# A third modulation piece is computed ahead of the attention, and its weight blocks move ahead of the output projection's

## The reference, cut to what matters

```
m = silu(cond) @ w_mod[l] + b_mod[l]            # (6 x 1024): m0..m5
h = x * (1 + m1) + m0
x = layer_norm(ALPHA * x + m2 * attention(h))
h = x * (1 + m4) + m3
x = layer_norm(ALPHA * x + m5 * moe(h))
```

## Time and profile before

| | us |
|---|---|
| Timed runs, median of 3 | 919.88 (914.09 to 920.38) |
| Profiled execution | 915.48 |
| Its span (first to last instruction) | 913.7 |
| TensorE busy, matmuls | 812.9 (89%) |
| VectorE busy | 277.4 (30%) |
| Transfers | 276.86 MB, mean 303 GB/s |

### The profile page before, as it was taken

The page is one execution under the profiler, slowest core; times in us unless marked ns, Lnnn a source line. Parts: engine busy times, 40 slices in busy tenths (PEclk is TensorE's granted clock), DMA queues, the critical chain, the costliest instruction groups (busy, mean ns, idle before and its releaser), DMA issues.

```text
span 913.7 us, 10159 instructions
## 1 busy us (share of the span) xinstructions
PE 812.9 (89%) x3883; PEld 396.2 (43%) x3883; DVE 277.4 (30%) x551; ACT 147.2 (16%) x384; POOL 82.3 (9%) x166
## 2 busy tenths in 40 slices
PE   3897988989899999999899957997789999999985
PEld 1454554464343434343234724546434443444321
DVE  0004444661121212221242074557112211221126
ACT  0201222231110111010021112323101010111101
POOL 0000000005110111000000030000511011100000
PEclk9798799999999999999999977997899999999998
DMA  8999902199979999999997099102098999999901
GB/s 314 352 356 401 387 30 92 64 410 422 369 312 421 412 416 420 425 416 417 387 365 263 14 411 422 66 32 93 2 366 331 424 411 422 408 428 418 376 0 47
DMA packets 66955, 276.86 MB, mean 303 GB/s; under 512 B 4668, under 2 KB 11324, under 8 KB 58724
## 3 DMA queue, kind: packets, MB, share of 16 engines
q1 hardware_dynamic: 65764, 275.59, 76.0%
q10 hardware_dynamic: 1152, 0.74, 0.3%
HBM read 274.79 MB, written 1.52 MB: 302 GB/s over the span
## 4 chain that ended last, share of the span: by engine, by line
PE 81%; DVE 9%; ACT 5%; DMA 2%; issue 2%; SPq 1%; POOL 1%; POOLq 0%; ACTq 0%; DVEq 0%
PE bank L952 24%; PE bank L1013 13%; PE bank L700 8%; PE bank L926 6%; PE bank L960 5%; PE bank L787 5%; PE bank L634 4%; PE bank L735 3%; DMA ring<-in_w_mod 2%; PE bank L613 2%; PE bank L766 2%; DVE arena L1410 2%; PE bank L744 2%; ACT arena L1469 1%; PE bank L934 1%
## 5 line engine op out<-in xcount | busy, mean ns | idle before, releaser
L952 PE MATMUL bank<-ring,arena 128*64 128x512 f32 x1024 | 226.2, 594 | 0.7 <-ACT arena L1469 0.7
L952 PEld LDWEIGHTS bank<-ring,arena 128*64 128x64 f32 x1024 | 75.3, 137 | 136.2 <-issue 135.3
L1013 PE MATMUL bank<-ring,arena 128*64 128x512 f32 x512 | 114.8, 601 | 11.9 <-ACT arena L1556 11.9
L1408 DVE TENSOR_SCALAR arena<-arena 128x256 f32<-128x256 f32 x32 | 9.4, 294 | 294.8 <-ACT arena L1543 294.8
L700 PE MATMUL bank<-ring,arena 128*128 128x512 f32 (+3 forms) x256 | 73.8, 450 | 2.6 <-ACT arena L1479 2.6
L926 PEld LDWEIGHTS bank<-arena 128*128 128x128 f32 x512 | 63.2, 196 | 22.8 <-issue 15.6
L1013 PEld LDWEIGHTS bank<-ring,arena 128*64 128x64 f32 x512 | 39.0, 138 | 77.5 <-issue 66.3
L1469 ACT ACTIVATE arena<-bank 128x512 f32<-128x512 f32 (+6 forms) x83 | 42.7, 531 | 178.9 <-PE bank L700 65.0
L926 PE MATMUL bank<-arena 128*128 128x128 f32 x512 | 64.9, 281 | 6.6 <-POOL arena L1673 5.2
L960 PE MATMUL bank<-arena 128*128 128x512 f32 x128 | 62.7, 615 | 0.0
L787 PE MATMUL bank<-ring,arena 128*128 128x512 f32 x128 | 60.0, 602 | 0.0
(11 more groups left out here) (151 smaller groups left out, 621.8 us busy)
## 6 DMA issues: line engine op xcount, KB each, us to landing
ring<-in_exp_w_gate SPq DMA_DIRECT2D x32, 2048.0 KB, 14.3
ring<-in_exp_w_up SPq DMA_DIRECT2D x32, 2048.0 KB, 15.2
ring<-in_exp_w_down SPq DMA_DIRECT2D x32, 2048.0 KB, 16.0
ring<-in_w_mod SPq DMA_DIRECT2D x24, 2048.0 KB, 18.0
ring<-in_w_out_ab SPq DMA_DIRECT2D x2, 2048.0 KB, 16.0
ring<-in_w_in_c SPq DMA_DIRECT2D x2, 2048.0 KB, 18.9
ring<-in_w_out_c SPq DMA_DIRECT2D x2, 2048.0 KB, 11.3
ring<-in_w_in_ab SPq DMA_DIRECT2D x1, 2048.0 KB, 19.5
```

The costliest lines, as they stand in the source:

```text
L952: mm = nc.tensor.matmul(pb(("gu", l))[SLOTS * hf:SLOTS * (hf + 1), :], xeT[b][:, k * P + SLOTS * a:k * P + SLOTS * (a + 1)], w[:, :, k, hf ...
L1013: mm = nc.tensor.matmul(pb(key)[SLOTS * a:SLOTS * (a + 1), :], hp[:, c:c + SLOTS], block_ap(n + 4 + a)[:, kf * D + hf * HALF: kf * D + (hf ...
```

## The change

The third modulation piece of layer 0 is computed right behind the second, ahead of the attention, in a bank of its own (bank 2). Its four blocks move ahead of w_out and lora in the stream; they are blocks 11 to 14, and w_out, lora, w_out become 15 to 17. The columns of the second modulation are turned behind the gates' broadcasts, ahead of the last output projection. VectorE adds the piece at the end of `normalise_even` and computes the scale and shift columns ahead of the residual steps of `layer_norm(0, 0)`. The two blocks that the third piece used to count as free are counted at the first transpose of `modulated(0, 1)`. At the end of layer 0 (s = 1) nothing moves.

```diff
@@ plan_blocks
-    order += [("mod", 0, c) for c in MOD_PIECES[1]] + [("wout", 0, 1), ("lora", 0, 0), ("wout", 0, 0)]
-    order += [("mod", 0, c) for c in MOD_PIECES[2]] + [("mod", 1, c) for c in MOD_PIECES[0]]
+    order += [("mod", 0, c) for p in (1, 2) for c in MOD_PIECES[p]]
+    order += [("wout", 0, 1), ("lora", 0, 0), ("wout", 0, 0)] + [("mod", 1, c) for c in MOD_PIECES[0]]
@@ plan_turns
                 if l == 0:
+                    t.use(("mod", 0, 2), 2)
...
-                t.use(("mod", s, 2 - s), 5)
                 if s == 0:
                     t.use(("modT", 0, 1), 5)
+                else:
+                    t.use(("mod", 1, 1), 5)
@@ TensorE: modulated
-                            if (l, s, g, q, k) == (1, 1, 0, 0, 0):
-                                mm.then_inc(blk_free, 1)
+                            if (s, g, q, k) == (1, 0, 0, 0):
+                                mm.then_inc(blk_free, 2 - l)
@@ TensorE: attention
                     if step == ("Y", len(units) - 1):
                         gates(l, 0)
+                        if l == 0:
+                            mod_columns(0, 1)
@@ TensorE: ln_rows
-            def ln_rows(l, s, free=0):
-                if l == 0:
-                    modulation(s, 2 - s, free)
+            def ln_rows(l, s):
+                if (l, s) == (0, 1):
+                    modulation(1, 1)
...
-                if (l, s) == (0, 0):
-                    pe.wait_ge(*saved(("mod", 0, 2)))
-                    mod_columns(0, 1)
@@ TensorE: the order of the layer
                 modulation(l, 1 + l, free=len(WIN[l]))
+                if l == 0:
+                    modulation(0, 2)
...
-                ln_rows(l, 0, free=2)
+                ln_rows(l, 0)
@@ VectorE: normalise_even, at its end
+                add_modulation(0, 2)
@@ VectorE: layer_norm
+                if (l, s) == (0, 0):
+                    mod_ab(0, 1)
                 add_up(0, 0)
...
-                if l == 0:
-                    add_modulation(s, 2 - s)
-                if (l, s) == (0, 0):
-                    mod_ab(0, 1)
+                if (l, s) == (0, 1):
+                    add_modulation(1, 1)
```

## The result

The changed kernel takes 936.0 us (median of 4 runs, 934.12 to 937.33) against 917.46 (914.09 to 920.38): a ratio of 1.0178 over the runs, with a 95% interval of 1.0128 to 1.0228 (the two medians alone would give 1.0202). It is slower by 18.5 us by the medians. The profiled execution took 936.17 us, its span 934.4 us, 20.7 more than the span of before.

| from | to | before, us | after, us | difference |
|---|---|---|---|---|
| start | second modulation piece | 71.9 | 73.4 | +1.5 |
| second piece | first scores | 13.4 | 32.6 | **+19.3** |
| first scores | gates' broadcasts | 85.2 | 84.8 | -0.5 |
| gates' broadcasts | router | 22.7 | 18.9 | **-3.8** |
| router | slot matmuls | 11.3 | 14.3 | **+3.0** |

What follows compares the result with a forecast made beforehand. TensorE was taken to bound the experts, transfers the first modulation piece. Scores 17.7 us later less 2.1 gained behind the attention gave 15.6 us more; on the median 919.88 that is 935.5, predicted 935, range 926 to 941.

Steps and rivals of the forecast that it cites:

- 1, the stream: Third piece's w_mod blocks land at about 76, 82.6, 87.7 and 93.2 us, at 5.4 us a block.
- 2, TensorE ahead of the attention: Third piece waits for its blocks and ends at 97.8 us at low clock; first scores 17.7 us later, at least 13.5.
- 3, the attention: Attention unchanged, w_out and lora blocks in time: nothing put down, bound 5.4 us if a load came late.
- 4, behind the attention: Third piece gone from the tail, but VectorE waits for the columns: 2.1 us gained, bound 4.8 or 8.0.
- 5, experts: Experts and layer 1: gain 0, as TensorE never waited for a block there.
- The first scores: Sign ahead of the attention: first scores at 99 to 103 us.
- The stretch from the gates to the slot matmuls: Sign in layer 0's tail: this stretch shorter by 2 to 5 us, VectorE's residual steps ending the wait.
- the stream's hole in the attention: Sign in the transfers: the stretch of nearly no transfers during layer 0's attention shorter by 20 us.
- A: Rival: third piece's blocks are there in time ahead of the attention; 1 to 3.5 us more, about 922; chance 0.07.
- B: Rival: the stream sets the experts' pace, so four blocks more ahead are worth 21 us; about 914.5; chance 0.03.
- C: Rival: same stall, but the clock stays high and the tail gives back all; about 925 to 928; chance 0.09.

Runs made afterwards that it cites:

- e4: The changed kernel with the modulation's columns turned ahead of the gates' broadcasts instead of behind them; 932.89 us, ratio to before 1.018.
- e5: e4 with idle TensorE filled by matmuls whose result nobody reads, in both layers; 926.36 us, ratio to before 1.0077.
- e3: The kernel before with only the changed block order in the stream, its order of computation kept; 924.58 us, ratio to before 1.0075.
- e1: The changed kernel, its third piece reading its first block four times, so without waits for the other three; 925.53 us, ratio to before 1.0076.

## Why the prediction was right, point by point

**The time** was in the range and within 1 us of 935, but the sum was 15.6 and the measured change 18.5 us. The time agrees better than the sum because I counted from 919.88, and the median of before with a fourth run is 917.46: the 2.4 us between them nearly cancel the 2.9 that the sum lacked. That the time is within 1 us is luck. The mechanism is the forecast one; two terms were mis-sized, the scores' delay (17.7 forecast, 19.3 measured) and what comes back behind the attention (2.1 and 0.9).

**1, the stream.** Right in kind: a step each 5.4 us. I put the last landing at 93.2 us; it was 95.8. The second piece starts 1.5 us later in this trace, but that doesn't explain the 2.6 us, as the landing doesn't follow that start: in e4 and e5 the last block's matmuls start at 94.43 and 95.09 us, with the second piece at 72.58 and 70.92. Most of the delay is there by the piece's second block (85.01, where I had 82.6); the block times behind it are the 5.4 us used. One reason shows in windows of the two traces, though no run tests it: from 68 to 84 us the transfers run at 402 to 409 GB/s in the kernel before, where w_out and lora pass, and at 387 to 391 with w_mod blocks in their place. Over 16 us that is 0.7 us, an estimate. The rate taken from the Trainium skill (DMA: Bandwidth & Descriptors, section "Bandwidth"), an estimated 4.9 us a block, was further off: the trace does not agree with it here.

**2, TensorE ahead of the attention.** The low clock was the right choice: 0.50 at 98 us. The last block and the bias took 5.5 us where I had 4.65 from the first piece, since here the whole run was at the low clock. The lead-in took 4.8 in place of 5.2. Scores 19.3 us later, relative to the second piece, in place of 17.7. The waits for w_mod were 1.7, 3.5 and 2.5 us, 7.6 together (6 to 8 forecast). That short runs between waits are run at the low clock is what the Trainium skill says (TensorE: Matmul & The Clock Gate, section "HAM oscillation — how this bites in real kernels"); the trace agrees in part, with 1.93, 2.96 and 3.64 us for equal runs: the run behind the first wait (1.7 us) was still at 1.00. How long the low clock lasts varies too: in e4 the bias took 1.04 and the lead-in up to the scores 3.2 us, which is the full clock, and its scores came 16.6 us later than before.

**3, the attention.** Nothing was late, -0.5 us. e3 shows that this zero was conditional: without the stall the same block order costs 7.3 us of waiting for lora. I looked only at the w_out block there, with a need at 101.6 us; lora's first use, at 96.7, was nearer. The stall hid the omission.

**4, behind the attention.** The first residual step came 5.7 us behind the start of the gates, as worked out (5.5). From there to the router 13.2 in place of 12.4 us: the transposes ran at the low clock too (1.97 us for 8 records, 1.09 in layer 1), behind 3.3 us in which TensorE idled ahead of the first of them, where layer 1 idles 0.4 (e4: 0.43 and 1.06 us for the 8 records). Router to slots took 14.3 us against 14.0 from the earlier trace rows. In all 0.9 us came back (33.1 us from the gates to the slot matmuls, in place of 34.0), not 2.1. Taking layer 1 as the model, and not layer 0's own full-clock router, was what made this small gain nearly right; e4 and e5 show its two causes apart, 2.9 us of wait and some 3 us of clock.

**5, experts.** No wait for a block, as said. The 1.3 us more come with one long run of down matmuls.

**Signs that were missed.** The first scores came at 106.1 us, outside 99 to 103 (in e4 and e5 inside). The stretch from the gates to the slot matmuls is 0.9 us shorter, and not 2 to 5. And I wrote that the stream's hole in the attention would be 20 us shorter. The SP queue does go on longer, with issues up to 122 us where they ended near 104, but the attention's end moved by some 20 us too, and the two places that the third piece freed at its start are now freed only at 204 us. With one block in its middle in both kernels, the hole goes from about 117 to 178 us before and from 137 to 204 us now: it is some 6 us longer. A lead gained by a stall is no lead.

**The rivals.** A (blocks in time) would have been 922; e1 makes it real and gives 925.5, the difference being the lora wait (1.5 us) and a tail that gives back 0.9 and not the 2.1 to 4.8 of the rival. B (the experts fed by the stream) fell, by the earlier trace rows and e3. C fell by the clock.

## What to carry to other kernels

Before work is moved ahead in a kernel with a streamed ring, read the landing time of its last block off the trace, from issues and times to landing, and also what stands behind it in the stream and when that is first needed; a hole in the stream later on is no reason by itself. Work that waits for blocks one by one is better laid out block by block into pauses at which each block is there (gates 0.9 us later here, in place of 20.3, for the same matmuls). And when work is taken out of a place in which TensorE waits for another engine, look at what runs behind the pause: a few matmuls for nobody saved 3 us there.

## What the runs showed of the hardware

Busy is not the same as fast: from 208 to 220 us of the changed kernel TensorE shows 2.00 busy of each 2.00 us, with the router's 16-column matmuls and with transposes, and the granted clock stays at 0.50 (1.2 GHz). It was back at 1.00 in the broadcasts of 512 columns that follow, at 222 us. The same router behind three 128x512 matmuls (2.74 us) ran at 1.00 from start to end, 3.64 us in place of 6.84. A pause is not needed for the clock to fall: in layer 1 of e5 TensorE works without a gap from 636.88 us on, and the granted clock is 0.80 from 641 to 642 us and 0.50 from 642 to 645; in the router of the kernel before (layer 0) it is 0.80 from 196 to 197 and 0.50 from 197 to 200 us, there and in the transposes behind it, the engine being busy since 193.19. What exactly the chip wants to see before it grants the full clock, these runs don't tell.
